# Gate and up products of a three-block network with both parts of the activations in one matmul of 512 columns

## What is computed

```
h = rms_norm(x, gain)                                         # 256 x 1024
x = x + (silu(h @ w_gate) * (h @ w_up)) @ w_down              # w_gate, w_up: 1024 x 2816, w_down: 2816 x 1024
```

## Time and profile before

| | |
|---|---|
| median of 3 runs | 1057.61 us (1054.39 to 1058.25) |
| profiled execution | 1057.54 us, its span 1055.4 us |
| TensorE busy | 1001.9 us (95%), 6886 matmuls |
| VectorE, ScalarE, GpSimd busy | 641.3 us (61%), 479.9 us (45%), 356.6 us (34%) |
| chain that ended last | TensorE 69%, VectorE 13%, GpSimd 6%, ScalarE 4%, DMA 3% |
| matmuls of 256 columns (L370, L371, L372) | 1232 of each |

### The profile page before, as it was taken

The page is one execution under the profiler, slowest core; times in us unless marked ns, Lnnn a source line. Parts: engine busy times, 40 slices in busy tenths (PEclk is TensorE's granted clock), DMA queues, the critical chain, the costliest instruction groups (busy, mean ns, idle before and its releaser), DMA issues.

```text
span 1055.4 us, 16844 instructions
## 1 busy us (share of the span) xinstructions
PE 1001.9 (95%) x6886; PEld 886.2 (84%) x6886; DVE 641.3 (61%) x650; ACT 479.9 (45%) x623; POOL 356.6 (34%) x325
## 2 busy tenths in 40 slices
PE   7999789999999988999999999999989999999997
PEld 5886579999987876787779999988866989999985
DVE  4799767666664446354656775544776665555544
ACT  4663435444434355546454434334533454443432
POOL 4790084888899604030009960000100010000000
PEclk9998789999999999999999999999999999999999
DMA  9542016677667755553355656556980455555540
GB/s 355 186 155 80 1 47 191 219 219 215 210 209 228 246 172 160 150 169 120 120 180 160 191 167 189 173 196 200 378 331 30 160 161 166 193 180 177 199 160 40
DMA packets 130033, 186.84 MB, mean 177 GB/s; under 512 B 4672, under 2 KB 103488, under 8 KB 129344
## 3 DMA queue, kind: packets, MB, share of 16 engines
q1 hardware_dynamic: 105696, 158.34, 46.0%
q10 hardware_dynamic: 24288, 27.81, 7.9%
HBM read 174.60 MB, written 15.73 MB: 180 GB/s over the span
## 4 chain that ended last, share of the span: by engine, by line
PE 69%; DVE 13%; POOL 6%; issue 4%; ACT 4%; DMA 3%; ACTq 0%; POOLq 0%; DVEq 0%; SPq 0%
PE ps L370 11%; PE ps L371 11%; PE ps L372 11%; PE ps L417 7%; PE ps L419 7%; PE ps L421 7%; DVE cacc L1748 4%; DVE wlo L354 3%; PE ps L389 3%; PE ps L391 3%; PE ps L390 3%; ACT whi L348 2%; POOL otmp L719 2%; DMA wraw<-in_s_w_glu 2%; POOL ob L733 2%
## 5 line engine op out<-in xcount | busy, mean ns | idle before, releaser
L354 DVE TENSOR_TENSOR wlo<-wraw,whi 128x2048 fp32r<-128x2048 f32 x145 | 354.2, 2443 | 241.8 <-ACT whi L348 241.8
L348 ACT ACTIVATE whi<-wraw 128x2048 fp32r<-128x2048 f32 x145 | 277.6, 1914 | 400.8 <-PE ps L372 224.6
L370 PE MATMUL ps<-actH,whi 128*128 128x256 f32 x1232 | 352.9, 286 | 5.4 <-DVE wlo L354 3.9
L371 PE MATMUL ps<-actL,whi 128*128 128x256 f32 x1232 | 349.9, 284 | 0.0
L372 PE MATMUL ps<-actH,wlo 128*128 128x256 f32 x1232 | 349.8, 284 | 0.0
L370 PEld LDWEIGHTS ps<-actH,whi 128*128 128x128 f32 x1232 | 237.3, 193 | 9.0 <-DVE wlo L354 4.5
L371 PEld LDWEIGHTS ps<-actL,whi 128*128 128x128 f32 x1232 | 237.4, 193 | 0.1
L372 PEld LDWEIGHTS ps<-actH,wlo 128*128 128x128 f32 x1232 | 237.4, 193 | 0.0
L559 POOL TENSOR_SCALAR rs<-ss 128x1 f32<-128x1 f32 (+2 forms) x16 | 6.1, 378 | 586.1 <-ACT nat L545 474.7
L417 PE MATMUL ps<-whi,gH 128*128 128x512 f32 x264 | 82.1, 392 | 0.0
L419 PE MATMUL ps<-wlo,gH 128*128 128x512 f32 x264 | 81.5, 390 | 0.0
(11 more groups left out here) (334 smaller groups left out, 1396.2 us busy)
## 6 DMA issues: line engine op xcount, KB each, us to landing
wraw<-in_ffn_w_gate SPq DMA_DIRECT2D x22, 1024.0 KB, 5.3
wraw<-in_ffn_w_up SPq DMA_DIRECT2D x22, 1024.0 KB, 5.4
wraw<-in_ffn_w_down SPq DMA_DIRECT2D x22, 1024.0 KB, 4.9
wraw<-in_fox_w_in SPq DMA_DIRECT2D x16, 1024.0 KB, 5.4
wraw<-in_w_gate SPq DMA_DIRECT2D x11, 1024.0 KB, 5.3
wraw<-in_w_up SPq DMA_DIRECT2D x11, 1024.0 KB, 5.7
wraw<-in_w_down SPq DMA_DIRECT2D x11, 1024.0 KB, 5.0
wraw<-in_w_in SPq DMA_DIRECT2D x10, 1024.0 KB, 7.9
```

The lines of the kernel that those rows point to most:

```text
L348: act.activation(self.whi[:, n0 % RING, :], self.wraw[:, n0 % RAW, :], ACT.Copy).then_inc(self.hi_done, 1)
L354: dve.tensor_tensor(self.wlo[:, n0 % RING, :], self.wraw[:, n0 % RAW, :], self.whi[:, n0 % RING, :].bitcast(F32), ALU.subtract).then_inc(s ...
L370: pe.matmul(out, wh, self.actH[:, k, :], start=(i == 0), stop=False)
L371: pe.matmul(out, wh, self.actL[:, k, :], start=False, stop=False)
```

## The change

`actH` and `actL` become the two halves of one tensor `act` (piece, part, token), so that both parts of a piece are 512 columns in a row. The new `mm_merged` multiplies the high weights with both in one matmul, into a whole PSUM bank for 128 features: high x high in columns 0 to 255, high x low in columns 256 to 511; low weights x high activations is added to the first half. A pair now fills four banks. Its two halves are summed on the way out: ScalarE copies the second half (`ghalf`, `uhalf`), VectorE adds the first (`gsum`, `usum`); the scaling and the product then read SBUF only. Pairs of f2 and f3 alternate between banks 4 to 7 and 0 to 3, those of f1 stay in 4 to 7, and its prep goes to banks 0 and 1. `over_pairs` issues three pairs alone and then four times two, with the prep ahead of a pair in the loop; ten preps lie between the pairs, six between the down units, after units 0, 2, 4, 6, 8 and 9.

```
+    def mm_merged(self, pe, n0, bank, it=0, ready=None, late=None, middle=None):
+        pe.wait_ge(self.lo_done, n0 + 4 * it + 1)
...
+        for f in range(2):
+            both, first_half = self.ps[:, bank + f, :], self.ps[:, bank + f, 0:TOK]
...
+                x = self.act[:, k].rearrange("p a t -> p (a t)")
+                if k == KT - 1:
+                    pe.matmul(first_half, wl, self.actH[:, k, :], start=False, stop=False)
+                    last = pe.matmul(both, wh, x, start=False, stop=True)
+                else:
+                    pe.matmul(both, wh, x, start=(k == 0), stop=False)
+                    pe.matmul(first_half, wl, self.actH[:, k, :], start=False, stop=False)
...
+    def pair_banks(self, st, f0):
+        return 4 if st == "f1" or f0 % 2 == 0 else 0
...
+        lag = 1 if st == "f1" else 2
+        b = self.pair_banks(st, f0)
+        if f0 >= lag:
+            pe.wait_ge(*self.past(st + "_gsum", f + 1 - lag))
+        self.mm_merged(pe, n0, b, it, ready, late)
+        if f0 >= lag:
+            pe.wait_ge(*self.past(st + "_usum", f + 1 - lag))
...
     def act_pair(self, act, st, n0, f0, it=0, f_step=0):
+        act.wait_ge(self.used, n0 + 4 * it + 1)
         if f0 > 0:
+            act.wait_ge(*self.past(st + "_prod", f))
+        act.activation(self.halves(self.sg), self.ps[:, b:b + 2, TOK:2 * TOK], ACT.Copy)\
+           .then_inc(self.sem(st + "_ghalf"), 1)
         self.split_high(act, n0 + 2, it)
...
         act.activation(self.sg[:], self.sg[:], ACT.Silu).then_inc(self.sem(st + "_silu"), 1)
+        act.wait_ge(self.used, n0 + 4 * it + 2)
+        if f0 > 0:
+            act.wait_ge(*self.past(st + "_glow", f))
+        act.activation(self.halves(self.prod), self.ps[:, b + 2:b + 4, TOK:2 * TOK], ACT.Copy)\
+           .then_inc(self.sem(st + "_uhalf"), 1)
         self.split_high(act, n0 + 3, it)
```

More of the change, by code:

```diff
@@ L32 @@
 FP = FT // 2
+PREP_DOWN = (0, 2, 4, 6, 8, 9)
 EPS = 1e-6
@@ L83 @@
         "sq": (("q", "k", "blk0", "blk1", "blk2", "blk3"), 2),
+        "ghalf": (("f1", "f2", "f3"), FP), "gsum": (("f1", "f2", "f3"), FP),
+        "uhalf": (("f1", "f2", "f3"), FP), "usum": (("f1", "f2", "f3"), FP),
         "gscaled": (("f1", "f2", "f3"), FP), "silu": (("f1", "f2", "f3"), FP), "prod": (("f1", "f2", "f3"), FP),
@@ L372, in mm_features @@
                 last = pe.matmul(out, wl, self.actH[:, k, :], start=False, stop=(i == KT - 1))
+            if f == 0 and middle:
+                middle()
+        last.then_inc(self.used, 1)
+    def mm_merged(self, pe, n0, bank, it=0, ready=None, late=None, middle=None):
+        pe.wait_ge(self.lo_done, n0 + 4 * it + 1)
+        s = n0 % RING
+        for f in range(2):
+            both, first_half = self.ps[:, bank + f, :], self.ps[:, bank + f, 0:TOK]
+            for k in range(KT):
+                if late and f == 0 and k in late:
+                    late[k]()
+                if ready is not None and f == 0:
+                    pe.wait_ge(*self.past(ready, k + 1))
+                c = k * 256 + f * P
+                wh, wl = self.whi[:, s, c:c + P], self.wlo[:, s, c:c + P]
+                x = self.act[:, k].rearrange("p a t -> p (a t)")
[5 more added lines that the diff above has]
+                    pe.matmul(first_half, wl, self.actH[:, k, :], start=False, stop=False)
             if f == 0 and middle:
@@ L651, in over_pairs, with pe_ffn @@
     def over_pairs(self, eng, one, prep=None):
-        one(0, 0, 0, 0)
-        if prep:
-            prep(0, 0, 0)
-        with eng.Fori(0, (FP - 1) // 2) as it:
+        for f in range(3):
+            one(2 * f, f, 0, 0)
+            if prep and f < 2:
+                prep(f, 0, 0)
+        with eng.Fori(0, (FP - 3) // 2) as it:
             for j in range(2):
-                one(2 + 2 * j, 1 + j, it, 2)
                 if prep:
-                    prep(1 + j, it, 2)
-    def pe_ffn(self, pe, st, a, late, prep=False):
+                    prep(2 + j, it, 2)
+                one(6 + 2 * j, 3 + j, it, 2)
+    def pe_ffn(self, pe, st, late, prep=False):
         n = self.first[st + ".up"]
+        base = 0
         act_ready = st + "_act_ready"
         self.over_pairs(pe, lambda dn, f0, it, fs: self.pe_pair(
-            pe, st, n + dn, a, f0, it, fs, act_ready if dn == 0 else None, late if dn == 0 else None),
-            (lambda b0, it, bs: self.pe_prep(pe, a, b0, it, bs)) if prep else None)
+            pe, st, n + dn, f0, it, fs, act_ready if dn == 0 else None, late if dn == 0 else None),
+            (lambda b0, it, bs: self.pe_prep(pe, base, b0, it, bs)) if prep else None)
         n = self.first[st + ".down"]
-        base = self.ffn_banks(a)[2]
+        if prep:
+            pe.wait_ge(*self.past("prep_rout", FP - 1))
+            pe.wait_ge(*self.past("prep_kout", FP - 1))
+        else:
+            pe.wait_ge(*self.past(st + "_gsum", FP - 1))
+            pe.wait_ge(*self.past(st + "_usum", FP - 1))
         for i in range(FT // 2):
@@ L675, in pe_ffn @@
                            first=st + "_first" if i == FT // 2 - 1 else None)
-            if prep and i % 2 == 1:
-                self.pe_prep(pe, a, FP + i // 2)
+            if prep and i in PREP_DOWN:
+                if i == 0:
+                    pe.wait_ge(*self.past(st + "_gsum", FP))
+                self.pe_prep(pe, 4, FP - 1 + PREP_DOWN.index(i))
     def expand_kernel(self, act, t):
@@ L747, in pe_prep @@
         for i in range(GB):
-            last = pe.matmul(self.ps[32 * i:32 * i + 32, a + 3, 0:P],
+            last = pe.matmul(self.ps[32 * i:32 * i + 32, a + 1, 0:P],
                              self.rtb[:, s, i, T - 2:T, :].rearrange("p t c -> p (t c)"),
@@ L1268, in _ @@
             late = m.pe_turn_plain(pe, "f1", "f1_x_ready", (0, 1, 2, 3, 6, 7), (0, 5))
-            m.pe_ffn(pe, "f1", 4, late, prep=True)
+            m.pe_ffn(pe, "f1", late, prep=True)
             pe.wait_ge(*m.past("prep_rout", NBLK))
@@ L1559, in _ @@
             m.act_pre_squares(act, "f1", "f1_x_ready")
-            m.act_ffn(act, "f1", 4, prep=True)
+            m.act_ffn(act, "f1", prep=True)
             for i in range(2):
```

85 lines of the change are left out of this document (43 added, 42 removed).

## The result

The change takes 1062.92 us in the median of 14 executions (1057.42 to 1070.67), the kernel before 1058.03 (1054.1 to 1060.3, 14 executions beside them): a ratio of 1.0057 [1.0039, 1.0075]. It is slower, by 4.9 us, where 0.3 less was forecast.

A forecast was written before the change was run, and what follows sets the result against it. TensorE was taken to bound f2 and f3, with GpSimd's table blocks a second bound in f1. f1 +2.1, f2 +2.2 and f3 -4.6 sum to -0.3 us on 1057.54: 1057.2 us, range 1046.5 to 1066.

The forecast's parts named there:

- Tiles of 347 ns: Gate and up products: a weight tile takes 347 ns instead of 360, so a pair saves 0.42 us.
- bounds of 0 and 13.8: Alternating 512 and 256 columns: 0 saved if each matmul after a 512 costs 13 ns more, 13.8 us by the rows.
- The rival that gave a tile 2.5 ns: All three blocks: tiles save only 2.5 ns, a pair 0.08 us, so 1065.3 us in all; chance 0.05.
- f3, -4.6: f3's gate and up products: 4.6 us shorter, bounds -5 and -3, with slack left on ScalarE and VectorE.
- f1's cycle: f1, two pairs and two GpSimd table blocks: 26.05 us instead of 25.57, GpSimd's block 12.4; f1 +2.1 us.
- Nothing there: f1's down products: the last table block is ready some 2 us before TensorE asks, so no cost.
- f2's waits: f2, beside GpSimd's phase tables: TensorE waits 8.1 us in place of 1.3; f2 +2.2 us, bounds -4.6 and +10.
- The clock: Granted clock of TensorE in f1, f2 and f3: read as 1.00 in all three; no term for a fall.
- little contention at all: f1 and f2: f2's waits also stay as they were, so -4.6 there and 1045.8 us in all; chance 0.14.
- free turns: f1: the two new VectorE instructions fall between GpSimd's, so -2.5 instead of +2.1, total 1052.6 us; chance 0.16.
- A third wlo in each f1 block: f1: one more wlo holds each GpSimd block 2.06 us, 10.3 over five cycles, total 1067.5 us; chance 0.14.
- The same within 0.1: Whole kernel: the profiled execution's 1057.54 us and the runs' median of 1057.61 were taken as the same.

The follow-up runs named there:

- f2_f3: Against the kernel before: f2 and f3 get the merged products, f1 keeps its old pairs, loop and preps; 1056.96 us, ratio 1.0003.
- stores_later: The change, with ScalarE's wait for f1's last table stores and its four loads moved into the next stage; 1062.03 us, 1.0045 to the kernel before.

## Why the prediction was wrong

The time was inside the range, and on the wrong side of no change. By its own steps:

- **Tiles of 347 ns: failed.** This is the step "227 + 120 by the two rows", which took each width's price from a stretch where that width stood alone. Mixed, a tile is 352.5. A pair saves 0.24 instead of 0.42, which over 33 pairs is 6 us; the 7.9 that are saved lie between the prediction's bounds of 0 and 13.8, and nothing on show before the run spoke for the upper one. The rival that gave a tile 2.5 ns by the formula of the Trainium skill (TensorE: Matmul & The Clock Gate, Back-to-back issue gap) was wrong too: 8 ns are saved.
- **f3, -4.6: sign right, size not.** -2.7, all of the error from the tile. ScalarE's and VectorE's slack held; there is no wait of TensorE on `wlo`. It fell just outside the bound of -3.
- **f1's cycle: right.** The block's 12.4 us were forecast and measured. 26.23 instead of 26.05 is the tile's 0.18. Forecast +2.1, and with the tile's error in it +3.1 to +3.2; measured +3.1. The agreement of the whole stage is in part luck, by the next step.
- **"Nothing there", the last blocks of f1: failed.** The prediction counted them ready 2 us ahead. GpSimd waits for stores for 4.26 and 2.18 us, and TensorE 0.72 for the last block; the down products with their preps are 2.0 us longer, 1.0 of which is the prep that the change moves there. The next stage's start came 1.5 sooner behind them than in before. 0.5 of that is the store, 2.65 us instead of 3.14; the rest is there because the chain leaves TensorE ahead of the last prep and runs over ScalarE's split, its copy of that prep and the store, so that the wait of 0.72 wasn't on it in this execution.
- **f2's waits: mechanism right, size too high.** 5.2 us instead of 8.1 (6.5 in `f2_f3` and `stores_later`, which have the same pairs in f2): the walk had waits in four pairs, the profile has three waits. Net of before +3.9 for +6.8 forecast, which gave back the tile's error of 2.0 and more; that f2 still took 3.0 us instead of 2.2 is the clock, next.
- **The clock: missing.** The prediction read 1.00 in all three blocks and kept it there, although it forecast waits of TensorE of 2.7 and 3.1 us in f2. A wait was priced at its own length; with a stretch behind it it costs some 1.5 us more, in some executions. Without it, tile and waits alone give -0.3 + 1.0 (f1) - 0.9 (f2) + 1.9 (f3) = +1.7 us. The 3 us of stretches, the mean of the three profiles, make it 4.7, and the medians give 4.9 and, the second time, 2.8. The sum closes better than its terms are known.
- **The rival on turns, "little contention at all", and "free turns": excluded** by the profile (cycle above 25.3). *A third wlo in each f1 block*: excluded too, the cycle is below 27.5. None of the rivals was what happened.
- **The median.** "The same within 0.1" held for the kernel before. For the change one profile stood 5.5 us below its own median, in stages that it doesn't touch and with a lucky clock. Its blocks alone were 3.4 us longer than before.

The turns themselves are confirmed by two runs from opposite sides, GpSimd's work taken away and the second SBUF operand taken away. The Trainium skill (SBUF — State Buffer, Who interferes with whom) has the rule that only VectorE's second pair of SBUF ports is shared with GpSimd, as an exclusive lock; the trace agrees, with 692 ns against 880 for both operands in SBUF, and 688 to 692 beside GpSimd's work with one in PSUM.

## What to carry to other kernels

Read what an instruction costs beside the neighbours that it will have: two prices from uniform stretches did not add up once the widths were mixed. When VectorE's work grows beside a busy GpSimd, count its instructions with both operands in SBUF, not its microseconds; sending a sum back to the PSUM bank, with the same number of instructions, took the ratio of this change from 1.0057 and 1.0036 to 0.9956. And price a wait of TensorE of the lengths seen here, 1.5 to 3 us, at its length plus a stretch at the lower clock that may follow (12 of 34 such waits, some 1.5 us each), which also means that one profile can't tell its cost.

## What the runs showed of the hardware that was not expected

- Matmuls of fp32 data with a weight load each: 120.0 ns at 256 columns alone, 226.7 at 512 alone, but 117.3 and 235.2 when they alternate (352.5 the pair), 118.6 and 233.0 in twos (351.6) and 119.1 and 230.1 in eights (349.2), where 346.7 would be the sum.
- The granted clock falls to half behind some waits of 1.5 us and not behind others of the same length in the same execution, nor behind two of 2.8 and 3.0. The Trainium skill (TensorE: Matmul & The Clock Gate, Part 1, What's actually happening) says of a kernel's first matmuls that how many run at the lower level differs from run to run of one kernel. No profile here was read for its first matmuls; in the middle of these blocks the stretches differ too, 1, 4 and 1 in three executions.
- Stages that were left alone are shorter or longer by up to 3 or 4 us with the time that they spend at the lower clock (the fox stage 173.0 us with none, 176.3 to 176.9 with 9 or 10 us of it).
- The last store of the tables takes 2.62 to 7.22 us from issue to landing, and a stage hung on it in both kernels.
